# Down weights of experts 2 to 29 asked for by ScalarE on its own DMA queue, gate and up weights by SyncE

## What is computed

```python
def hier_moe(h, w_rg, b_rg, w_re, b_re, w_gate, w_up, w_down):
    t = h.reshape(-1, D_MODEL)                      # 256 tokens x 2048
    ...                                             # top-1 group, then top-2 experts in it
    combine = jnp.sum(jax.nn.one_hot(ids, N_EXPERTS, dtype=jnp.float32) * w_sel[..., None], axis=1)
    y = jnp.zeros((n_tok, D_MODEL), jnp.float32)
    for e in range(N_EXPERTS):                      # 32 experts
        a = jax.nn.silu(t @ w_gate[e]) * (t @ w_up[e])              # 2048 -> 512
        y = y + combine[:, e:e + 1] * (a @ w_down[e]).astype(jnp.float32)   # 512 -> 2048
    return y.astype(h.dtype).reshape(h.shape)
```

## Time and profile before

| | |
|---|---|
| times of three runs | 2287.23, 2283.2 and 2288.18 us, median 2287.23 us |
| the profiled execution | 2282.66 us |
| its span, first to last instruction | 2280.9 us |
| PE busy | 2150.7 us, 94% of the span |
| DVE busy | 1381.5 us, 61% |
| ACT busy | 730.3 us, 32% |
| mean granted TensorE clock | 0.984 of full speed |
| HBM read | 756.12 MB |
| SyncE's queue q1 | 758.31 MB, 82.9% of the time of 16 DMA engines |
| ScalarE's queue q10 | 0.79 MB, 0.1% |

### The profile page before, as it was taken

The page is one execution under the profiler, slowest core; times in us unless marked ns, Lnnn a source line. Parts: engine busy times, 40 slices in busy tenths (PEclk is TensorE's granted clock), DMA queues, the critical chain, the costliest instruction groups (busy, mean ns, idle before and its releaser), DMA issues. The chain is left out here.

```text
span 2280.9 us, 35465 instructions
## 1 busy us (share of the span) xinstructions
PE 2150.7 (94%) x14337; PEld 1634.9 (72%) x14337; DVE 1381.5 (61%) x2196; ACT 730.3 (32%) x1324; POOL 39.9 (2%) x62
## 2 busy tenths in 40 slices
PE   8999999999999999899999979999999998899996
PEld 7899999888999998788898754555454544454552
DVE  6988889988888899755556463333333333333334
ACT  6544555455444554556555320000000000000001
POOL 0010000000000000120000000000000000000000
PEclk9999999999999999999999989999999999999998
DMA  9988777988887779654444389999999999999997
GB/s 351 372 341 322 279 260 279 363 334 347 326 325 279 258 280 377 235 212 156 138 149 150 128 326 422 432 431 432 432 431 432 432 432 430 431 432 432 431 428 297
DMA packets 70200, 760.75 MB, mean 334 GB/s; under 512 B 7968, under 2 KB 10944, under 8 KB 13632
## 3 DMA queue, kind: packets, MB, share of 16 engines
q1 hardware_dynamic: 69936, 758.31, 82.9%
q10 hardware_dynamic: 144, 0.79, 0.1%
HBM read 756.12 MB, written 2.95 MB: 333 GB/s over the span
## 5 line engine op out<-in xcount | busy, mean ns | idle before, releaser
L1233 DVE TENSOR_TENSOR s_w_tail<-s_raw,s_w_head 128x1024 fp32r<-128x1024 f32 x292 | 345.0, 1222 | 17.6 <-ACT s_w_head L835 17.3
L1023 PE MATMUL b_ps<-s_h_head,s_w_head 128*128 128x256 f32 x1184 | 341.0, 288 | 0.0
L835 ACT ACTIVATE s_w_head<-s_raw 128x1024 fp32r<-128x1024 f32 x292 | 294.4, 1051 | 143.3 <-DMA s_raw<-in_w 92.6
L1024 PE MATMUL b_ps<-s_h_tail,s_w_head 128*128 128x256 f32 x1184 | 334.8, 283 | 0.0
L1025 PE MATMUL b_ps<-s_h_head,s_w_tail 128*128 128x256 f32 x1184 | 334.8, 283 | 0.0
L1348 DVE CUSTOM_DVE_ANT_0 s_raw<-s_raw,s_c_row 128x2048 f32<-128x2048 f32 x128 | 292.2, 2283 | 0.2
L1023 PEld LDWEIGHTS b_ps<-s_h_head,s_w_head 128*128 128x128 f32 x1184 | 226.7, 192 | 4.2 <-issue 3.9
L1024 PEld LDWEIGHTS b_ps<-s_h_tail,s_w_head 128*128 128x128 f32 x1184 | 227.0, 192 | 0.2
L1025 PEld LDWEIGHTS b_ps<-s_h_head,s_w_tail 128*128 128x128 f32 x1184 | 226.8, 192 | 0.0
L2445 ACT ACTIVATE s_hidden<-b_ps 128x256 f32<-128x256 f32 x32 | 12.3, 383 | 627.6 <-PE b_ps L2505 627.6
L2752 DVE TENSOR_TENSOR s_y<-b_ps,s_gate_row 128x512 f32<-128x512 f32 x64 | 44.3, 692 | 231.9 <-PE b_ps L2529 231.9
(11 more groups left out here) (360 smaller groups left out, 3569.4 us busy)
## 6 DMA issues: line engine op xcount, KB each, us to landing
s_raw<-in_w SPq DMA_DIRECT2D x198, 1024.0 KB, 5.5
s_raw<-in_w_ada SPq DMA_DIRECT2D x128, 1024.0 KB, 6.4
s_third_slot<-in_w_gate SPq DMA_DIRECT2D x7, 4096.0 KB, 31.5
s_last_slot<-in_w_up SPq DMA_DIRECT2D x7, 4096.0 KB, 29.6
first_slot<-in_w_down SPq DMA_DIRECT2D x7, 4096.0 KB, 31.7
s_second_slot<-in_w_gate SPq DMA_DIRECT2D x7, 4096.0 KB, 29.8
s_third_slot<-in_w_up SPq DMA_DIRECT2D x7, 4096.0 KB, 27.6
s_last_slot<-in_w_down SPq DMA_DIRECT2D x7, 4096.0 KB, 30.4
```

The lines of the kernel that those rows point to most:

```text
L835: act.activation(w_head[:, g % SPLITS, cols], raw[:, ring, cols], ACT.Copy)\
L1023: pe.matmul(out, head, m_head, start=first, stop=False, skip_group_check=True)
L1024: pe.matmul(out, head, m_tail, start=False, stop=False, skip_group_check=True)
L1233: dve.tensor_tensor(w_tail[:, g % SPLITS, cols], raw[:, slot["w", g], cols], w_head[:, g % SPLITS, cols].bitcast(F32), ALU.subtract)\
```

## The change

ScalarE issues the down pieces of experts 2 to 29 (28 of the 96 pieces) on its own queue. SyncE's loop keeps gate and up. The down pieces of experts 0, 1, 30 and 31 stay with SyncE. The wait before the DMA is the same count of `used`, but on ScalarE it stands behind the copy into `hidden_t` of the expert before. As the buffer of a piece has to be known when the kernel is built, ScalarE's loop now goes over four experts a turn (experts 1 to 28), with expert 0 and experts 29 to 31 written out. What TensorE, VectorE and GpSimd do is unchanged.

```diff
-    def load_whole(sp, e, c, slot):
-        src = (w_gate, w_up, w_down)[c][bass.ds(e, 1), :, :].rearrange("a p n -> (a p) n")
-        sp.dma_start(ring[slot].rearrange("p c n -> p (c n)"), src).then_inc(arrived[slot][0], 16)
+    def load_whole(eng, e, c, slot):
+        pick_e = bass.ds(e, 1) if not isinstance(e, int) else slice(e, e + 1)
+        src = (w_gate, w_up, w_down)[c][pick_e, :, :].rearrange("a p n -> (a p) n")
+        eng.dma_start(ring[slot].rearrange("p c n -> p (c n)"), src).then_inc(arrived[slot][0], 16)
...
             with sp.Fori(0, EXPERTS // 4 - 1) as four:
                 for j in range(4):
-                    for c in range(PIECES_E):
+                    for c in range(2):
                         seq = PIECES_E * (j + 2) + c
                         sp.wait_ge(sem["used"], four * (4 * USED_E) + (2 * (seq - SLOTS_E) + 2))
                         load_whole(sp, four * 4 + (j + 2), c, seq % SLOTS_E)
...
-            with act.Fori(0, EXPERTS) as e:
+            def one_expert(j, four=None):
+                def of(each, n):
+                    return j * each + n if four is None else four * (4 * each) + (j * each + n)
+                column = own[:, j:j + 1] if four is None else own[:, bass.ds(four * 4 + j, 1)]
...
+                act.wait_ge(sem["turned"], of(2, 2))
                 act.activation(hidden_t[:, :, :].rearrange("p a c -> p (a c)"), psum[:, 3, 0:2 * P], ACT.Copy)\
                    .then_inc(sem["hidden_t"], 1)
+                if four is not None:
+                    act.wait_ge(sem["used"], of(USED_E, 4))
+                    load_whole(act, four * 4 + (j + 1), 2, (PIECES_E * (j + 1) + 2) % SLOTS_E)
+
+            one_expert(0)
+            with act.Fori(0, EXPERTS // 4 - 1) as four:
+                for j in range(1, 5):
+                    one_expert(j, four)
+            for j in (EXPERTS - 3, EXPERTS - 2, EXPERTS - 1):
+                one_expert(j)
```

More of the change, by code:

```diff
@@ L2442, in _ @@
         with act.Else():
-            with act.Fori(0, EXPERTS) as e:
-                act.wait_ge(sem["used"], e * USED_E + 2)
+            def one_expert(j, four=None):
+                def of(each, n):
+                    return j * each + n if four is None else four * (4 * each) + (j * each + n)
+                column = own[:, j:j + 1] if four is None else own[:, bass.ds(four * 4 + j, 1)]
+                act.wait_ge(sem["used"], of(USED_E, 2))
                 act.activation(hidden[:, 0, :], psum[:, 0, 0:T], ACT.Exp, scale=-1.0)\
                    .then_inc(sem["gate_exp"], 1)
-                act.wait_ge(sem["turned"], e * 2 + 1)
-                act.activation(weigh_t[:, :], psum[:, 2, 0:T], ACT.Copy, scale=own[:, bass.ds(e, 1)])\
+                act.wait_ge(sem["turned"], of(2, 1))
+                act.activation(weigh_t[:, :], psum[:, 2, 0:T], ACT.Copy, scale=column)\
                    .then_inc(sem["weights_t"], 1)
-                act.wait_ge(sem["turned"], e * 2 + 2)
+                act.wait_ge(sem["turned"], of(2, 2))
                 act.activation(hidden_t[:, :, :].rearrange("p a c -> p (a c)"), psum[:, 3, 0:2 * P], ACT.Copy)\
                    .then_inc(sem["hidden_t"], 1)
+                if four is not None:
[7 more added lines that the diff above has]
+                one_expert(j)
             for t in range(TT):
```

## The result

| | before | changed |
|---|---|---|
| median of 15 runs | 2286.05 us | 2293.38 us |
| lowest to highest | 2283.2 to 2289.77 | 2287.79 to 2294.65 |
| profiled execution, span | 2280.9 us | 2287.8 us |

The ratio is 1.003, 95% interval 1.0023 to 1.0037: the change makes the kernel slower by 0.23% to 0.37%. The ratio is worked out from all fast runs of both kernels; it is not the ratio of the two medians, and can differ from it by a us or two. Forecast was +8 us and 2295 us.

What follows compares the result with a forecast made beforehand. The prediction took DMA transfers at 431 GB/s to bound the kernel. Up of expert 29 landing one piece later gave +7.3 us, +9.0 with a clock fall, taken as +8: 2287.2 + 8 = 2295 us, range 2284 to 2303.

Steps and rivals of the forecast that it cites:

- What bounds the kernel: Stage of the experts: from near 1600 us transfers set the pace at 431 GB/s, 29.2 us per expert, queue never dry.
- SyncE's issues, ScalarE's issues and loop: nothing: SyncE loses 28 issues of 0.33 us, ScalarE gains 28 hidden by 19 us of waiting; loop by four: all worth nothing.
- Equal turns: SyncE's and ScalarE's DMA queues get about equal time where both are filled; +8 us (bounds +4 and +11), chance 0.62.
- A down piece lands after 20.5 us and overtakes its up piece: Alone in ScalarE's queue, down lands 20.5 us after issue, not 30 to 32, before its expert's up, issued 7 us earlier.
- Up of 29 lands at 2196.9, one piece later: End of the stage: six pieces instead of seven land after up of expert 29, so 2196.9 instead of 2187.1 us.
- TensorE's tail: After up of expert 29 TensorE runs at its own pace; last scatter products at 2267.0 against 2259.70, +7.3 us.
- the case without the fall: TensorE's clock does not fall at the wait for up of expert 29: +7.3 us; with a fall +9.0.
- Waits of 2 to 3 us on every second expert: TensorE's DMA waits move to up pieces, 2 to 3 us every second expert, hardly any at the down product.
- The range: Predicted median time of the whole kernel: 2284 to 2303 us, taking in no change and a slightly lower rate.
- No change in order: Rival: transfers served nearly in order of issue, or TensorE's lead absorbs the difference; 2287 us, chance 0.20.
- A higher rate: Rival: two queues raise the rate above 431 GB/s; 2279 to 2284 us, or 2291 with a small gain; chance 0.08.
- Unequal turns: Rival: SyncE's queue gets three turns for one, down takes 39 us; +15 to +45 us; slower-still chance 0.10.

Runs made afterwards that it cites:

- experiment 2: Against the kernel before: ScalarE issues the down pieces of experts 2 to 25 only, SyncE those of 26 to 29; 2284.89 us, ratio 1.0000.
- experiment 1: Against the kernel before: ScalarE's loop goes over four experts, SyncE still issues all pieces; 2284.60 us, ratio 0.9999.
- experiment 4: As the changed kernel, but ScalarE issues the down piece ahead of its two copies; 2292.90 us, ratio 1.0031 against the kernel before.
- experiment 9: Against the kernel before: ScalarE issues all pieces of experts 2 to 31 and the two loads of final-norm rows; 2286.09 us, ratio 1.0001.
- experiment 7: As the changed kernel, but ScalarE asks for each down piece in two halves, rows 16 KB; 2299.15 us, ratio 1.0061 against the kernel before.
- experiment 5: Against the kernel before: ScalarE issues only the down piece of expert 29, SyncE the other 95 pieces; 2290.21 us, ratio 1.0030.
- experiment 3: Against the kernel before: ScalarE issues only the down pieces of experts 26 to 29, SyncE all others; 2292.41 us, ratio 1.0028.
- experiment 10: Against the kernel before: all weights on SyncE's queue, ScalarE issues only the two loads of final-norm rows; 2290.96 us, ratio 1.0022.
- experiment 6: Against the kernel before: ScalarE issues all pieces of experts 2 to 31, SyncE still loads the final-norm rows; 2292.90 us, ratio 1.0032.

## Why the prediction was right, step by step

*What bounds the kernel.* Right. Transfers set the pace and never stop. The last weights of the changed kernel land at the same time (2257.4 and 2257.5 us), and experiment 2 has the disturbed order for 24 experts at no cost.

*SyncE's issues, ScalarE's issues and loop: nothing.* Right, by experiments 1, 4 and 9. The first shows the loop, the second the moment of the issue, the third 90 of the 96 pieces issued by ScalarE. The ratios leave room for some 2 us either way.

*Equal turns.* Right, and now shown where both queues are full. A down piece is issued by ScalarE at 2147.34. The queues from there, in the changed kernel (packets, MB, share): first 2147.3 to 2150.3, then 2150.3 to 2152.3, then 2152.3 to 2160 us.

```profile
q1 hardware_dynamic: 40, 1.21, 93.9%
...
q10 hardware_dynamic: 16, 0.52, 61.0%
q1 hardware_dynamic: 12, 0.39, 45.7%
...
q10 hardware_dynamic: 51, 1.67, 50.4%
q1 hardware_dynamic: 52, 1.61, 48.4%
```

For 3 us after the issue q10 has no packet; then both queues send packets at the same pace, 51 and 52 in the last stretch. Experiment 7 tells by what the turns go. There ScalarE's packets are 16 KB and SyncE's 32 KB; this is a stretch in which both queues are full, from 1965 to 1974 us, and behind it one of those in which SyncE's is empty, 2022 to 2025 us:

```profile
q10 hardware_dynamic: 78, 1.26, 32.9%
q1 hardware_dynamic: 80, 2.62, 67.6%
...
q10 hardware_dynamic: 90, 1.29, 101.4%
```

With about as many packets (78 and 80) ScalarE's queue moves half the bytes and has 33% of the time. Turns go by packet, as the Trainium skill says ("DMA: Bandwidth & Descriptors", Queues, rings and completion order). What the profile counts as a packet is one row of a piece, 32 or 16 KB; whether a turn is one such packet or several is not shown. By the sentence of the Trainium skill on the same page (Issuing engines are not separate DMA queues) that issuing from several engines saves only the time to issue, there would have been no change; here the time rose by 0.3%, as the order of landing changed.

*A down piece lands after 20.5 us and overtakes its up piece.* Off by 2.8 us. It takes 23.3 us. Some 2 us of the difference are its start, 3 us after the issue and not 1 as I had counted (the earlier trace rows already had such 3 us for ScalarE's earlier DMA); the rest is not accounted for. So down of 29 lands at 2176.50 + 22.6 = 2199.1, 1.8 us behind up of 29 (2197.3) and not ahead. In the changed kernel, then, down of 29 does not overtake up of 29 whole: what is left of it when up lands is 1.8 us of transfers, about a fifth of a piece. Experiment 5 has the whole overtaking.

*Up of 29 lands at 2196.9, one piece later.* Measured 2197.3, 10.2 us later than before; 2197.4 with one piece moved (experiment 5). That the forecast is so close is in part luck. Its 2255.6 us for the last landing takes 32.3 us for the last quarter, but that is the median over four quarters; the last one takes 34.1 us and lands at 2257.4. From there six pieces at 9.73 us lead back to 2199.0, 2 us later than forecast, and that is where down of 29 landed (2199.1). Up of 29 came 1.8 us ahead of it, as the overtaking was not whole. The two errors, each near 2 us, cancel. The mechanism stands without them: 10.2 us is about one piece.

*TensorE's tail.* The last scatter products were forecast at 2267.0 without a fall of the clock and 1.7 us later with one, and began at 2267.28. There was no fall: the first product after the wait took 7.15 us, and the granted clock of the stretch is 1.00. The forecast of +8 was the middle of these two cases. The one without the fall gives +7.3, and the profiled execution had +7.6 there. The one with it gives +9.0, and the executions of experiments 3 and 4 are of that kind: their stage was 10.0 and 8.6 us longer. The profiled execution of the changed kernel (2289.68 us) is one of five between 2287.8 and 2289.7 us; the other ten took 2292.2 to 2294.7 us, and no trace tells whether the clock fell in them. So the median's +7.3 agrees with the case without the fall, but is not shown to come from it.

*Waits of 2 to 3 us on every second expert.* Wrong in form: 1.7 us on each of them, somewhat more in sum. It changes nothing in the time.

*The range.* 2284 to 2303 us also takes in no change, so the time alone proves little; the landings and experiments 2, 3, 5, 9 and 10 carry the argument.

*The rivals.* No change in order: excluded by the landings. A higher rate: 431 GB/s in both kernels, though q10 had 33.3% of the time; two queues moved no more than one. Unequal turns: not in the changed kernel, but experiment 7 made them, and the price, 13.9 us by the medians and 10.4 in the profiled executions, is somewhat below the +15 at the low end of that rival.

*What stays open.* The trace does not say what the 3 us before the first packet of a second queue are. Nor is it shown what decides whether the clock falls at such a wait: it fell behind waits of 2.9 and 3.0 us for up of 29 (experiments 4 and 3), not behind 1.8 and 2.4 us (the changed kernel and experiment 5), but in the kernel before it fell behind one of 1.72 us.

## What to carry to other kernels

Where transfers set the pace, as here at 431 GB/s, a second DMA queue brought no rate; here it changed the order in which things land, by equal turns of packets. That cost nothing measurable in the middle of the stream (experiment 2) and was paid at its end, where the consumer has to work off what came late: so keep the last few transfers in one queue in the order of their use, and look for every small load that gets a queue of its own beside them. When a number fits a rival, as in experiment 6, look for what else your edit left in the other queue before you believe it.

## What was not expected of the hardware

A single 4 MB DMA in the other queue, of 760 MB moved, was worth 0.30%, 6.9 us by the ratio (experiment 5). And 2 MB of row loads, which nobody waits for until the very end, cost 5 us by their queue alone (experiment 10), which is about what their own bytes take at 431 GB/s (4.9 us).
